# One-core transformer block in Bass: moving squares, sums and weight splits around the four norm boundaries

## The reference

```python
u = rmsnorm(h, ffn1_pre);  h = h + 0.5 * rmsnorm(swiglu(u, Wg, Wu, Wd), ffn1_post)   # d_ff 2816
u = rmsnorm(h, mix_pre);   z = u @ w_in                      # attention and mLSTM branches
h = h + rmsnorm((g_a * a + g_b * bm) @ w_out, mix_post)
u = rmsnorm(h, ffn2_pre);  h = h + 0.5 * rmsnorm(swiglu(u, ...), ffn2_post)
e = p @ w_proj;  g = sigmoid(rmsnorm(h, ple_pre) @ w_gate);  h = h + rmsnorm(g * e, ple_post)
# rmsnorm(x, w) = x * rsqrt(mean(x * x over the width) + 1e-6) * w
```

## Time and profile before

| what | value |
|---|---|
| time, median of 3 runs | 1301.32 us (1300.29 to 1301.88) |
| the profiled execution: time / span | 1301.57 us / 1299.7 us |
| TensorE busy | 1254.9 us, 97% of the span, mean granted clock 0.981 |
| VectorE, ScalarE, GpSimd busy | 675.6 (52%), 424.3 (33%), 118.5 us (9%) |
| HBM traffic over the span | 82 GB/s |
| chain that ended last | PE 84%, DVE 7%, issue 4%, ACT 2%, POOL 2% |

### The profile page before, as it was taken

How to read it: one execution, slowest core, us unless ns; L and a number is a source line. 1 busy time by engine, 2 the same in 40 slices (tenths; PEclk the granted TensorE clock), 3 DMA queues, 4 the chain that set the end, 5 groups by cost and what they waited for, 6 DMA issues and landing times.

```text
span 1299.7 us, 15628 instructions
## 1 busy us (share of the span) xinstructions
PE 1254.9 (97%) x5910; PEld 1033.9 (80%) x5910; DVE 675.6 (52%) x1043; ACT 424.3 (33%) x612; POOL 118.5 (9%) x96
## 2 busy tenths in 40 slices
PE   7999999999989999999999999899999999999996
PEld 6888888888867867777788878778888888888785
DVE  6644444442257866646446486485444443222774
ACT  5323232311134343435411433243232322112552
POOL 3000000000024000001101200230000000000343
PEclk9999999999989999999999999899999999999997
DMA  5433333232222321110311123214232323333101
GB/s 190 130 98 96 97 97 97 97 97 97 97 59 49 100 79 34 33 37 30 114 49 49 33 89 107 65 50 128 83 110 82 112 81 112 97 97 111 52 17 65
DMA packets 96866, 107.75 MB, mean 83 GB/s; under 512 B 15062, under 2 KB 87478, under 8 KB 96822
## 3 DMA queue, kind: packets, MB, share of 16 engines
q1 hardware_dynamic: 96608, 107.10, 26.5%
q10 hardware_dynamic: 214, 0.05, 0.0%
HBM read 105.04 MB, written 2.10 MB: 82 GB/s over the span
## 4 chain that ended last, share of the span: by engine, by line
PE 84%; DVE 7%; issue 4%; ACT 2%; POOL 2%; DMA 0%; SPq 0%; DVEq 0%; POOLq 0%; ACTq 0%
PE bank L283 24%; PE bank L285 23%; PE bank L284 23%; PE bank L879 2%; PE bank L893 2%; DVE v_lo L456 1%; PE bank L411 1%; PE bank L512 1%; DVE tbuf L449 1%; PE bank L507 1%; PE bank L901 1%; PE bank L377 1%; PE bank L508 1%; PE bank L290 1%; POOL sqacc L397 1%
## 5 line engine op out<-in xcount | busy, mean ns | idle before, releaser
L313 DVE TENSOR_TENSOR w_lo<-w_raw,w_hi 128x1024 fp32r<-128x1024 f32 x195 | 241.9, 1246 | 374.0 <-ACT w_hi L306 366.8
L283 PE MATMUL bank<-v_hi,w_hi 128*128 128x512 f32 x968 | 381.3, 394 | 0.3 <-ACT og L1396 0.3
L285 PE MATMUL bank<-v_hi,w_lo 128*128 128x512 f32 x968 | 377.4, 390 | 0.0
L284 PE MATMUL bank<-v_lo,w_hi 128*128 128x512 f32 x968 | 377.2, 390 | 0.0
L306 ACT ACTIVATE w_hi<-w_raw 128x1024 fp32r<-128x1024 f32 x195 | 203.8, 1054 | 364.3 <-PE bank L285 360.7
L285 PEld LDWEIGHTS bank<-v_hi,w_lo 128*128 128x128 f32 x968 | 182.0, 188 | 38.4
L283 PEld LDWEIGHTS bank<-v_hi,w_hi 128*128 128x128 f32 x968 | 182.2, 188 | 38.0 <-ACT og L1396 0.5
L284 PEld LDWEIGHTS bank<-v_lo,w_hi 128*128 128x128 f32 x968 | 182.2, 188 | 37.6 <-issue 0.2
L285 PE MATMUL bank<-prod_hi,w_lo 128*128 (+1 forms) x352 | 136.9, 389 | 0.0
L283 PE MATMUL bank<-prod_hi,w_hi 128*128 (+1 forms) x352 | 136.9, 389 | 0.0
L284 PE MATMUL bank<-prod_lo,w_hi 128*128 (+1 forms) x352 | 136.9, 389 | 0.0
(11 more groups left out here) (271 smaller groups left out, 1405.8 us busy)
## 6 DMA issues: line engine op xcount, KB each, us to landing
w_raw<-in_ffn_w_gate SPq DMA_DIRECT2D x44, 512.0 KB, 3.6
w_raw<-in_ffn_w_up SPq DMA_DIRECT2D x44, 512.0 KB, 3.5
w_raw<-in_ffn_w_down SPq DMA_DIRECT2D x44, 512.0 KB, 3.4
w_raw<-in_w_in SPq DMA_DIRECT2D x32, 512.0 KB, 3.7
w_raw<-in_w_out SPq DMA_DIRECT2D x8, 512.0 KB, 3.2
w_raw<-in_ple_w_gate SPq DMA_DIRECT2D x8, 512.0 KB, 3.3
x_tm<-in_x SPq DMA_DIRECT2D x4, 512.0 KB, 7.3
w_raw<-in_w_branch_mla SPq DMA_DIRECT2D x4, 512.0 KB, 3.3
```

Source lines behind the costliest of these rows:

```text
L283: nc.tensor.matmul(o, whi, a_hi, start=start, stop=False)
L284: nc.tensor.matmul(o, whi, a_lo, start=False, stop=False)
L285: return nc.tensor.matmul(o, wlo, a_hi, start=False, stop=stop)
L313: nc.vector.tensor_tensor(w_lo[:, s, :], w_raw[:, s, :], w_hi[:, s, :].bitcast(F32), ALU.subtract).then_inc(w_lo_done, 1)
```

## The change

It moves work at the boundaries and in the leads. Squares of `y` go to ACT, which reads PSUM; DVE only copies, after ACT. `ADDED` becomes a number for each boundary (five squares added by POOL at 1 to 3, six at the last norm), and `H_ADDED` = 6 replaces the eight additions of `h` squares, the last two squares getting ones-matmuls of their own. One group of `y` sums stands before the last eighth of the products. In the mixer's last chunk the two output banks are finished one after the other. In the leads, two chunks are worked on together, tile by tile. w_lo of chunk N+2 goes behind the first rsqrt, w_lo of N+3 before tile 3, w_hi of N+3 before all tiles (at boundary 3 the placements differ, see the end). The DVE and ACT programs of boundary 0 are not touched.

```diff
-ADDED = 6
+ADDED = [0, 5, 5, 5, 6]
+H_ADDED = 6
-    def token_sums(o, src):
+    def token_sums(o, src, start, stop):
         for tb in range(TB):
-            last = nc.tensor.matmul(..., ones[:, 0:1], start=True, stop=True)
+            last = nc.tensor.matmul(..., ones[:, 0:1], start=(start and tb == 0), stop=stop, skip_group_check=True)
...
+    def y_sum_first(pe, n):
+        b = bs[n]
+        b.wait(pe, "y_copied", 1)
+        b.wait(pe, "ysq_act", ADDED[n] + 1)
+        token_sums(B[YBANK[0]], scratch[:, ADDED[n] % 4, :], True, False)
+
+    def y_sum_rest(pe, n):
+        b = bs[n]
+        b.wait(pe, "y_acc", ADDED[n])
+        token_sums(B[YBANK[0]], sqacc[:], False, False)
+        for p in range(ADDED[n] + 1, KD):
+            b.wait(pe, "ysq_act", p + 1)
+            last = token_sums(B[YBANK[0]], scratch[:, p % 4, :], False, p == KD - 1)
+        last.then_inc(b["y_sum"], 1)
...
+    def y_copy_dve(dve, n, p, ready):
+        ready(dve, p)
+        bs[n].wait(dve, "ysq_act", p + 1)
+        nc.vector.tensor_copy(ys[:, p, :], ybank(p)).then_inc(bs[n]["y_copied"], 1)
+
+    def y_square_act(act, n, p, ready):
+        ready(act, p)
+        if p >= 4:
+            b.wait(act, "y_acc", p - 3)
+        nc.scalar.activation(scratch[:, p % 4, :], ybank(p), ACT.Square).then_inc(b["ysq_act"], 1)
...
-    def boundary_dve(dve, n, post, pre):
+    def boundary_dve(dve, n, post, pre, N):
         post_norm_dve(dve, n)
+        lo_upto(dve, N + 2)
+        bs[n].wait(dve, "r1b_ready", 1)
         for m in range(KD):
+            if m == 3:
+                lo_upto(dve, N + 3)
             h_tile_dve(dve, n, m, post)
...
     def lead_pe(pe, n, N, after_first=None):
+        def chunks(k, js):
+            for j in js:
+                if k % 4 == 0:
+                    pe.wait_ge(w_lo_done, N + j + 1)
+            b.wait(pe, "vhi_ready", max(k + 1, 2) if n == 0 else k + 1)
+            ... (for j in js, f in 0, 1: whi*v_hi[k], wlo*v_hi[k])
+            b.wait(pe, "v_ready", k + 1)
+            ... (for j in js, f in 0, 1: whi*v_lo[k]; after k = 3 and 7: then_inc(w_used, 1) for each j)
+        if n == 0:
+            for k in range(4):
+                chunks(k, [0])
+            after_first()
+            for k in range(4):
+                chunks(k, [1])
+        elif n == 3:
+            for k in range(2):
+                chunks(k, [0])
+            pe.wait_ge(ps["e_out"], 8)
+            for k in range(2):
+                chunks(k, [1])
+            for k in range(2, 4):
+                chunks(k, [0, 1])
+        else:
+            for k in range(4):
+                chunks(k, [0, 1])
+        for k in range(4, 6):
+            chunks(k, [2, 3])
+        for k in range(6, KD):
+            chunks(k, [2])
+        b.wait(pe, "h_acc", H_ADDED)
+        token_sums(B[HSTAT_BANK], sqacc[:], True, False)
+        for m in range(H_ADDED, KD):
+            b.wait(pe, "hsq_ready", m + 1)
+            last = token_sums(B[HSTAT_BANK], scratch[:, m % 4, :], False, m == KD - 1)
+        last.then_inc(b["h2_ready"], 1)
+        for k in range(6, KD):
+            chunks(k, [3])
...  # the tail of the down product, m from 0 to 7
                 if m < KD - 1:
                     last.then_inc(yb["y_ready"], 1)
+                if m == KD - 2:
+                    y_sum_first(pe, n + 1)
...  # last chunk of the product with w_out
-            fm_pair(pe, WO + j, half, [YBANK[2 * g], YBANK[2 * g + 1]], v_hi, v_lo, KD)
+            if j < 7:
+                fm_pair(pe, WO + j, half, [YBANK[2 * g], YBANK[2 * g + 1]], v_hi, v_lo, KD)
+        pe.wait_ge(w_lo_done, WO + 8)
+        for f in range(2):
+            for kk in range(4):
+                c = kk * 256 + f * P
+                last = three(B[YBANK[6 + f]][:], wv(WO + 7, c, c + P), v_hi[:, 4 + kk, :], v_lo[:, 4 + kk, :], False, kk == 3)
+            last.then_inc(bs[2]["y_ready"] if f == 0 else w_used, 1)
+            if f == 0:
+                y_sum_first(pe, 2)
...  # y_wo, the wait ahead of the copy and square of a tile of boundary 2
+            if p == 6:
+                bs[2].wait(eng, "y_ready", 1)
+            else:
+                after(eng, WO + (2 + p // 2 if p < 4 else 2 * (p // 2) + 1))
...  # DVE at boundary 3
         for m in range(KD):
-            if m == 4:
-                lo_upto(dve, EP + 4)
+            if m in (3, 4):
+                lo_upto(dve, PG + m - 1)
...  # ACT
-        hi_upto(act, CQ + 2)
+        hi_upto(act, CQ + 3)
...
-        hi_upto(act, UP2 + 2)
+        hi_upto(act, UP2 + 3)
...
-        v_tiles_act(act, 3, gain("ple_pre_norm"), {3: lambda: e_act(act, 1)})
+        v_tiles_act(act, 3, gain("ple_pre_norm"), {2: lambda: e_act(act, 1), 4: lambda: hi_upto(act, PG + 3)})
```

More of the change, by code:

```diff
@@ L379, in bcast_rows @@
         return last
-    def token_sums(o, src):
+    def token_sums(o, src, start, stop):
         for tb in range(TB):
-            last = nc.tensor.matmul(o[:, tb:tb + 1], src[:, tb * P:(tb + 1) * P], ones[:, 0:1], start=True, stop=True)
+            last = nc.tensor.matmul(o[:, tb:tb + 1], src[:, tb * P:(tb + 1) * P], ones[:, 0:1], start=(start and tb == 0),
+                                    stop=stop, skip_group_check=True)
         return last
@@ L397, in y_squares_pool, with out_sums_pe @@
             nc.gpsimd.tensor_tensor(sqacc[:], sqacc[:], scratch[:, p % 4, :], ALU.add).then_inc(b["y_acc"], 1)
-    def y_sums_pe(pe, n, bank):
+    def y_sum_first(pe, n):
         b = bs[n]
[L402 to L412, removed]
+        b.wait(pe, "y_copied", 1)
[9 more added lines that the diff above has]
+        last.then_inc(b["y_sum"], 1)
+    def out_sums_pe(pe):
+        b = bs[4]
+        b.wait(pe, "y_acc", ADDED[4])
+        token_sums(B[SUMS], sqacc[:], True, False)
+        for p in range(ADDED[4], KD):
+            b.wait(pe, "ysq_act", p + 1)
+            last = token_sums(B[SUMS], scratch[:, p % 4, :], False, p == KD - 1)
         last.then_inc(b["y_sum"], 1)
@@ L422, in boundary_pe @@
         b.wait(pe, "r1_ready", 1)
+        b.wait(pe, "y_copied", KD)
         bcast_rows(B[R1_BANK], r1c).then_inc(b["r1b_ready"], 1)
@@ L480, in h_squares_pool @@
         b = bs[n]
-        for m in range(KD):
+        for m in range(H_ADDED):
             b.wait(pool, "hsq_ready", m + 1)
@@ new lines, in chunks @@
+        def chunks(k, js):
[3 more added lines that the diff above has]
+            b.wait(pe, "vhi_ready", max(k + 1, 2) if n == 0 else k + 1)
+            for j in js:
+                for f in range(2):
+                    c = (k % 4) * 256 + f * P
+                    o, (whi, wlo) = B[4 + 2 * (j % 2) + f], wv(N + j, c, c + P)
+                    nc.tensor.matmul(o[:], whi, v_hi[:, k, :], start=(k == 0), stop=False)
+                    nc.tensor.matmul(o[:], wlo, v_hi[:, k, :], start=False, stop=False)
+            b.wait(pe, "v_ready", k + 1)
+            for j in js:
+                for f in range(2):
+                    c = (k % 4) * 256 + f * P
+                    last = nc.tensor.matmul(B[4 + 2 * (j % 2) + f][:], wv(N + j, c, c + P)[0], v_lo[:, k, :], start=False,
+                                            stop=(k == KD - 1))
+                if k % 4 == 3:
+                    last.then_inc(w_used, 1)
@@ L1325, in mixer_act @@
         lead_act(act, 1, CQ)
-        bs[1].wait(act, "h_acc", KD)
+        bs[1].wait(act, "h2_ready", 1)
         for t in range(4):
@@ L1490, in p_transposes_pe @@
         pe.wait_ge(p_in, 32)
-        bs[3].wait(pe, "ysq_dve", 1)
-        bs[3].wait(pe, "ysq_act", 2)
+        bs[3].wait(pe, "y_copied", 3)
+        bs[3].wait(pe, "ysq_act", 3)
         for k in range(2):
@@ L1697, in _ @@
         h_squares_pool(pool, 0)
-        for p in range(ADDED):
+        for p in range(ADDED[1]):
             y_squares_pool(pool, 1, p)
```

91 lines of the change are left out of this document (28 added, 63 removed).

## The result

The changed kernel takes **1311.38 us** (median of 4 runs, 1310.53 to 1311.63); the kernel before, on the same chip, 1301.6 us (1300.29 to 1302.43). The ratio is 1.0075, 95% interval 1.0057 to 1.0092. Forecast was 1307.0 us with a range from 1303.6 to 1309.9: the sign was right, the size was not, and the time lies outside the range. The profiled execution took 1311.24 us, its span is 1309.4 us, 9.7 more than before.

What follows compares the result with a forecast made beforehand. TensorE, busy 97% of the span, was taken to bound the kernel, so only its waits, extra work and low clock count. +8.96 - 1.4 - 0.7 - 0.5 - 0.7 = +5.7 us on 1301.32 gave 1307.0, range 1303.6 to 1309.9.

Steps and rivals of the forecast that it cites:

- Boundary 0: First lead: PE waits 4.85 us for w_lo of chunk 3, low-clock restart 2.49, two more h-sum groups 1.62: +8.96 us.
- the relief of v_lo: Boundary 0: without POOL's addition beside it, v_lo of tile 5 shortens from 1.77 us; what follows comes 1.03 us earlier.
- Boundary 1, y sums: Sums before lead 1: one woven group and earlier POOL additions let the sums end at 379.99, gaining 1.4 us.
- Leads 1 and 2: Leads of boundaries 1 and 2: 2.3 us of idle time goes, two h-sum groups take back 1.62; gain 0.7 each.
- Lead 3: Lead of boundary 3: the 1.89 us wait goes, broadcast at 1251.1 plus 0.4 against 1252.27; -1.1 us.
- The mixer: Y sums ahead of boundary 2: a woven group of 0.91 us, then three groups, ending at 835.46 against 835.28; cost 0.2.
- Feed-forward 2 and the tail: Y sums of boundary 3: +0.91 us for the group, -0.48 for the wait, so +0.4; last product and tail 0.
- A: Rival: boundary 0 loses only the 1.62 us of sums, as w_lo of chunk 3 is ready; 1299.6 us, chance 0.06.
- B: Rival: the clock does not fall at boundary 0 and stays high at boundaries 1 and 2; 1300.1 us, chance 0.06.
- D: Rival: the weave fails, PE waits at `y_sum_first` for a square, at most 1.36 us at two places; 1309.7, chance 0.06.
- C: Rival: POOL's relief fails (+1.0) and w_lo of N+3 in VectorE's chain eats the leads' gains (+2.1); 1310.1 us, chance 0.12.

Runs made afterwards that it cites:

- The base: The changed kernel with one group of h sums in each lead (H_ADDED = 8) and the old chunk order at boundary 0: 1294.35 us, ratio 0.9943.

## Why the forecast was wrong

- **Boundary 0: right.** +8.61 against +8.96. The wait is the 4.85 us that were forecast, the relief of v_lo came, and with the old order there the wait is gone. The restart at the low level was 4.8 us long for twelve matmuls (30.33 to 35.14), so it cost 2.0 us instead of 2.49. No low stretch follows the three groups at 40.61, which was luck: with the old order one does (21.15 us instead of 19.3), and the forecast had no term for it.
- **Boundary 1, y sums: right in sum, wrong in cause.** -1.35 against -1.4, and the sums end 3.0 us after the last product's start, as forecast. The forecast let one woven group and POOL's five additions remove the wait; the run with six additions and no woven group shows that the squares on ACT are enough for it, gaining 2.3, and that the weave costs 1.0.
- **Leads 1 and 2: the step that failed.** The forecast had each lead 0.7 shorter: 2.3 from the waits, less 1.62 for two more groups. The base, with one group, shows the 2.3 exactly (29.74 and 29.77 against 32.06 and 32.05), and a second group costs 0.7. But in "the two groups of h sums take back 1.62" the groups were priced by their duration alone. Here each run of 24 was followed by a low stretch, 1.6 us more. Instead of -0.7 the leads measured +0.65 and +0.61, and 0.3 of the slow broadcast stands after them. The broadcast of lead 1 came 30.6 us after the first tile (392.47 to 423.07) and not 29.3. With products between the groups the same leads take 31.56 and 31.67, with 24 in one run 32.71 and 32.66.
- **Lead 3: the same, and a wait that stayed.** Forecast -1.1, measured +1.81. The low stretch is there too (34.74, and 33.24 with the groups spread). And even with one group the lead is only 0.4 shorter than before. PE still waits for v_lo, 1.22 and 0.61 us in the base (1.89 before), so following DVE "instruction by instruction" gave v_lo too early. PE of the base in lead 3:

```profile
1231.35 1.19 PE L529 MATMUL bank<-v_lo,w_hi 128*128 128x512 f32 x4 [1.22 <-DVE v_lo L471]
...
1239.88 0.74 PE L529 MATMUL bank<-v_lo,w_hi 128*128 128x512 f32 x2 [0.61 <-DVE v_lo L471]
```

- **The mixer: only its y sums (+0.2) were in the forecast.** +2.86, nearly all clock: the window at the q sums is at 0.77 instead of 0.89, and one near 605 at 0.72 instead of 1.00. No instruction there was changed. What brings it is open. It was gone with the groups spread (422.15) and came with the two extra groups in before (424.27), which would blame the groups. But it was mostly gone with all runs of 24 in place and the old order at boundary 0 (422.68), and whole with one group in each lead and the wait at boundary 0 left (424.33).
- **Given back: feed-forward 2 and the tail, -1.09 and -1.70.** In before the clock is low behind the y sums of boundary 3, in after it isn't; in the tail it falls later. Nothing in the change aims at either, so the time would have been further off without them.

By sum: the forecast had +5.7, the profile +9.7. The leads account for +5.6 of the difference, the mixer for +2.7, the last two for -3.2, boundary 0 and the arrival of x for -1.0. So the step that failed is the price of the h sums in the leads, with the wait in lead 3, and behind it the clock of the mixer, which the forecast put at nothing without a reason.

Rivals A, B and D did not happen. C came nearest (1310.1), for the wrong reason: the relief came and no split was late at boundary 1 or 2. B looked at the clock but only for a gain; nothing in the forecast asked whether a longer run of thin matmuls could cost it. The rows for that question were there. In before, the mixer's run of 32 is followed by a low stretch, while the single group of the earlier trace rows is not:

```profile
427.64 3.73 PE L824 MATMUL bank<-ones,scratch 128*128 128x1 f32 x32
...
431.81 0.63 PE L284 MATMUL bank<-v_lo,w_hi 128*128 128x512 f32 x1
```

What stays open is which runs of sums are followed by a low stretch. Over all profiles: in the leads, 10 of 14 runs of 24 were (not boundary 0 of the changed kernel in either profile, not lead 2 with the old order at boundary 0, nor lead 2 of the kernel before with added groups), and none of the sums in the other 50 leads, with runs of 8, of 16 or spread groups. The mixer's run of 32 was in all 13 profiles that have it. The y sums of boundary 3, also 24 in one run with matmuls on both sides, were in 7 of 16 profiles.

There the run and what stands around it can be ruled out as the whole cause. The base and the kernel without the weave at boundary 2 alone have the same instructions for over 350 us ahead of these sums. The base (feed-forward 2 in 348.16 us) goes on at full pace behind them, the other (349.76 us) does not:

```profile
1205.86 1.93 PE L385 MATMUL bank<-ones,scratch 128*128 128x1 f32 x16
...
1208.42 0.40 PE L284 MATMUL bank<-pT_hi,w_hi 128*128 128x512 f32 x1
```

```profile
1202.99 1.93 PE L385 MATMUL bank<-ones,scratch 128*128 128x1 f32 x16
...
1205.92 0.63 PE L284 MATMUL bank<-pT_hi,w_hi 128*128 128x512 f32 x1
```

So a run of 24 makes a low stretch possible and not certain. A rival that is left for the rest is the moment in the execution at which the run comes: every edit ahead of it also moves it in time. The second profile of the changed kernel ran 1.1 us later with the same low stretches; no run here moved the sums further and changed nothing else.

## What to carry to other kernels

Price a thin matmul (one column of results, as in the sums) not only by its time but by what it may do to the clock. Keep such runs short, or put dense matmuls between them, if nothing waits for the sums. Look in the old profile for the longest run of them and what follows it. Compare low stretches over more than one profile before an edit is blamed for one. When two chunks are worked on together, the second one's operands are needed one chunk earlier; check every place where the loop is used, above all the one whose producers were not moved. And test the parts alone: with one constant (the eight additions left to POOL) and one loop bound (at boundary 0) put back, the same change is 0.6% faster than before instead of 0.75% slower.

## What the runs showed of the hardware

- The granted clock fell with TensorE never idle: 24 ones-matmuls of 2.6 us in all, dense matmuls on both sides, and half pace soon behind them, which cost 1.6 us (0.83 in the window of lead 1, changed kernel). The Trainium skill ("TensorE: Matmul & The Clock Gate", section "Why this matters for your kernels") warns of idle gaps between bursts of matmuls; this case shows that a fall can follow thin work without a gap, too.
- Two profiles of one kernel had the low stretches at the same work, though x arrived 1.1 us apart; the pieces from the first broadcast on differ by at most 0.2 us. Two kernels with the same instructions around a run of 24 had a low stretch behind it in one and not in the other (0.63 and 0.40 above).
- With the groups spread in the changed kernel, low stretches went in some places and stood in others: of 6.2 us won in four pieces, 2.8 were lost in two others. A gain in the clock has to be read off the whole span.
